# FFN gate and up projections: the low part of a weight chunk formed by an adding transfer instead of by VectorE

## What is computed

```python
def swiglu(h, w_gate, w_up, w_down):
    return (jax.nn.silu(h @ w_gate) * (h @ w_up)) @ w_down
...
        x = x + y
        x = x + swiglu(rms_norm(x, norm_ffn[i]), w_ffn_gate[i], w_ffn_up[i], w_ffn_down[i])
```

## Time and profile before

| what | value |
|---|---|
| time, median of 3 runs | 1503.15 us (1502.79 to 1503.18) |
| span of the profiled execution, first to last instruction | 1500.0 us |
| TensorE busy in the span | 1469.1 us, 98% |
| VectorE, ScalarE, GpSimd busy | 49%, 32%, 14% |
| mean busy share of the 16 DMA engines in a stretch of gate/up (220 to 440 us) | 0.26 |
| granted TensorE clock, mean of the span | 0.993 |

### The profile page before, as it was taken

One profiled execution on the slowest core, in us unless ns is written; L12 is line 12 of the kernel. 1 busy time (PEld: TensorE's weight loads), 2 busy tenths in 40 slices (PEclk: granted clock), 3 DMA queues, 4 the chain that ended last, 5 costly groups with the idle time before them and its releaser, 6 DMA issues.

```text
span 1500.0 us, 28016 instructions
## 1 busy us (share of the span) xinstructions
PE 1469.1 (98%) x11754; PEld 1426.6 (95%) x11754; DVE 728.8 (49%) x867; ACT 475.5 (32%) x547; POOL 208.4 (14%) x209
## 2 busy tenths in 40 slices
PE   6999999999999999999999999989999999999997
PEld 5989999999999999988989989979999999999997
DVE  6564544444443333465574773875444444443223
ACT  3432232222222212254263362463222222221111
POOL 6011130000000112014013041041210000000221
PEclk9999999999999999999999999999999999999998
DMA  6212122222222222555254263333222222222221
GB/s 236 85 61 93 54 88 85 84 97 99 84 75 77 95 97 90 219 175 183 85 204 154 98 232 111 140 140 142 85 99 99 84 84 98 97 66 78 96 97 57
DMA packets 32230, 165.84 MB, mean 111 GB/s; under 512 B 3904, under 2 KB 6224, under 8 KB 20400
## 3 DMA queue, kind: packets, MB, share of 16 engines
q1 hardware_dynamic: 21792, 126.90, 24.3%
q0 software_dynamic: 10384, 38.16, 7.1%
HBM read 140.46 MB, written 24.59 MB: 110 GB/s over the span
## 4 chain that ended last, share of the span: by engine, by line
PE 95%; DVE 2%; ACT 1%; POOL 1%; issue 0%; DMA 0%; DVEq 0%; SPq 0%; ACTq 0%; POOLq 0%
PE ps L1361 83%; PE ax L1722 2%; PE ax L1731 1%; PE ax L1704 1%; PE ps L1862 1%; PE ax L1651 1%; PE ax L1743 1%; PE ax L1379 1%; PE ax L1387 1%; DVE h_lo L711 1%; PE ax L1689 0%; PE ax L1530 0%; POOL acc L1233 0%; PE ax L1499 0%; DMA x<-in_x 0%
## 5 line engine op out<-in xcount | busy, mean ns | idle before, releaser
L1361 PE MATMUL ps<-h_hi,whi 128*128 128x260 f32 x2432 | 496.8, 285 | 1.3 <-DVE wlo L731 1.3
L1361 PE MATMUL ps<-h_hi,wlo 128*128 128x260 f32 x2432 | 491.1, 284 | 0.0
L1361 PE MATMUL ps<-h_lo,whi 128*128 128x260 f32 x2432 | 490.1, 283 | 0.0
L1361 PEld LDWEIGHTS ps<-h_hi,whi 128*128 128x128 f32 x2432 | 376.4, 189 | 8.0 <-issue 4.9
L1361 PEld LDWEIGHTS ps<-h_hi,wlo 128*128 128x128 f32 x2432 | 375.9, 189 | 0.0
L1361 PEld LDWEIGHTS ps<-h_lo,whi 128*128 128x128 f32 x2432 | 375.4, 189 | 0.0
L351 ACT ACTIVATE whi<-raw 128x2048 fp32r<-128x2048 f32 (+1 forms) x119 | 210.6, 1770 | 490.4 <-PE ps L1361 481.9
L706 DVE TENSOR_TENSOR wlo<-raw,whi 128x2048 fp32r<-128x2048 f32 (+1 forms) x119 | 255.5, 2147 | 128.9 <-ACT whi L351 128.7
L722 DVE TENSOR_TENSOR t<-ps,rstd 128x520 f32<-128x520 f32 x108 | 75.5, 699 | 274.8 <-PE ps L1361 269.1
L1361 PE MATMUL ps<-hid_hi,whi 128*128 128x260 f32 x660 | 133.2, 283 | 0.0
L1361 PE MATMUL ps<-hid_hi,wlo 128*128 128x260 f32 x660 | 132.7, 282 | 0.0
(11 more groups left out here) (260 smaller groups left out, 1587.6 us busy)
## 6 DMA issues: line engine op xcount, KB each, us to landing
raw<-in_w_f SPq DMA_DIRECT2D x44, 1024.0 KB, 4.7
raw<-in_w_oi SPq DMA_DIRECT2D x24, 1024.0 KB, 4.7
raw<-in_w_d SPq DMA_DIRECT2D x32, 704.0 KB, 4.0
sring<-in_ret_in POOLq DMA_DIRECT2D x32, 512.0 KB, 4.8
out_ret_s<-sring POOLq DMA_DIRECT2D x32, 512.0 KB, 3.0
raw<-in_w_e SPq DMA_DIRECT2D x8, 1024.0 KB, 4.7
raw<-in_w_oo SPq DMA_DIRECT2D x8, 1024.0 KB, 4.7
raw<-in_w_eo SPq DMA_DIRECT2D x4, 1024.0 KB, 4.7
```

Source lines behind the costliest of these rows:

```text
L1361: ins = pe.matmul(dst[t], lhs(a, kw), rhs[b][:, kx, HT * t:HT * t + HT], start=(first and n == 0 and q == 0), stop=(last and n == len(ks_) ...
```

## The change

For the 20 chunks that are formed inside the gate/up loop of each layer (n = 0 to 19, forming chunks 2 to 21), VectorE's subtraction is left out. ScalarE first writes the negated high part into `wlo` (a copy of `raw` with scale -1, rounded on writing) and after it the high part into `whi`. GpSimd waits for the negated part and issues a transfer that adds `raw` onto `wlo` where it lies, so that `wlo` ends as `raw` minus the high part. VectorE, at the place where it subtracted, waits for that transfer, tells TensorE that the low part is there, and goes on with `hid_lo`. All other chunks keep the subtraction. The core of the diff:

```diff
+        s_neg = sem("ffn_weights_hi_negated")
+        s_sum = [sem(f"ffn_weights_lo{i}_summed") for i in range(2)]
...
                         act.activation(t1[:], t0[:], ACT.Silu).then_inc(s_sg, 1)
+                        if size == W_FULL:
+                            act.wait_ge(s_raw[j], 8 * (c0 + n + 2 - j) + 16)
+                            act.wait_ge(s_mm, m0 + 2 * n + 2)
+                            act.activation(wlo[j][:], raw[j][:], ACT.Copy, scale=-1.0).then_inc(s_neg, 1)
                         hi(c0 + n + 2, j, size, (s_mm, m0 + 2 * n + 2))
...
                         dve.tensor_tensor(t3[:], t2[:], t1[:], ALU.mult).then_inc(s_hid, 1)
-                        lo(c0 + n + 2, j, size)
+                        if size == W_FULL:
+                            dve.wait_ge(s_whi, c0 + n + 3)
+                            dve.wait_ge(s_sum[j], 16 * ((FT // 2 - 1) * l + i + 1))
+                            dve.sem_inc(s_wlo, 1)
+                        else:
+                            lo(c0 + n + 2, j, size)
                         dve.wait_ge(s_hidhi, g + 1)
...
+            def ffn_lo(l):
+
+                with pool.Fori(0, FT // 2 - 1) as i:
+                    for j in range(2):
+                        pool.wait_ge(s_neg, (FT - 2) * l + 2 * i + j + 1)
+                        pool.sem_inc(s_pstep, 1)
+                        pool.dma_start(wlo[j][:].bitcast(F32), raw[j][:], accum_op=ALU.add).then_inc(s_sum[j], 16)
+
             for n, m0 in ((1, M_EO), (2, M_D[0])):
                 for m in range(KT):
                     squares(n, m, (s_out, m0 + m + 1))
+                if n == 1:
+                    ffn_lo(0)
...
+                if n == 3:
+                    ffn_lo(1)
```

## The result

The changed kernel takes **1509.28 us** (median of 8, 1504.85 to 1510.27), the kernel before 1503.29 (median of 8, 1502.79 to 1504.70): a ratio of 1.0030, 95% interval 1.0021 to 1.0039. It is slower, by 6 us in the medians where 19 were forecast (the changed kernel's executions spread over 5.4 us; the means, 1508.16 and 1503.46, are 4.7 apart, and the ratio lies nearer to theirs). Of the kernels further down, one execution of the late wait (2396.86 us) and one of negation first (3672.16 us) lie far above all others; the medians in the table hold them and the ratios do not. The profiled execution took 1504.99 us with a span of 1503.5, so 1.5 us lie around the span.

The account below looks back on a forecast made before the run. TensorE, busy 98% of the span, was taken to bound the kernel. A ring of 12.02 us against 11.54 over 40 chunks gave +19 on the 1500.0 span, 1519, plus 3.15 to the median: 1522 us, range 1501 to 1600.

Parts of the forecast that it names:

- What bounds the kernel, and what the removal buys: In gate/up TensorE alone bounds, 11.54 us per chunk; removing 92 us of VectorE subtractions buys nothing.
- The ring: Gate/up loop per chunk: negating copy, GpSimd, transfer, hid_lo, gate tile, SiLU; 4.62 us + X against TensorE's 11.54.
- X: Adding transfer's time from issue to landing in gate/up; free up to 6.92 us, beyond that 40 us per us.
- I take 7.4: Chosen adding-transfer time in us, a quarter of the way from 6.9 to 9.0; 0.48 over per chunk, +19 us.
- my middle line: Adding transfer with second read at the first's pace: 6.9 us; ring 11.52, a hair under TensorE's 11.54.
- hidden: Rival: adding transfer in gate/up takes at most 7.0 us and costs nothing; 1503 us, chance 33%.
- 7.3 us of slack: Before the change, VectorE's low part in gate/up is ready 7.3 us before TensorE wants the slot again.
- No margin at all: Argument against the hidden rival: the ring at 6.9 just fits, and hand-overs counted at 0.03 us may be more.
- the likeliest case: The ring binds in gate/up, X between 7.0 and 9.0 us; 1506 to 1586, likeliest 1522; chance 50%.
- The frame: Around the whole kernel: the runs' median lies 3.15 us above the span, taking 1519 to 1522 us.

Follow-up runs that it names:

- late wait: Changed kernel with VectorE's wait for the adding transfer moved behind the next chunk's gate tile; 1503.35 us, ratio 1.000 to the kernel before.
- negation first: Changed kernel with ScalarE's negating copy placed ahead of the same chunk's SiLU; 1508.40 us, ratio 1.0038 to the kernel before.
- plain copy: Changed kernel with GpSimd's transfer copying raw over wlo instead of adding; 1506.34 us, ratio 1.0024 to the kernel before; run again 1504.40 us, 1.0009.
- the half: Changed kernel with only 1024 of 2048 columns negated and transferred, VectorE subtracting the others after the wait; 1504.02 us, ratio 1.0009 to the kernel before.
- third-pair kernel: Changed kernel with the first two pairs of chunks of each layer keeping VectorE's subtraction; 1505.13 us, ratio 1.0016 to the kernel before.

## Why the prediction was right and wrong

- **What bounds the kernel, and what the removal buys: right.** The subtractions stood on no path; 92 us less on VectorE quickened nothing, and the late-wait kernel, which has the same relief, is at 1.000.
- **The ring: right in its path and its slope; its length is right partly by luck.** TensorE waits for the gate tile, and adding 0.53 us to the ring cost 20 us. Without X it was put at 4.62, and it measures 11.56 - 6.93 = 4.63. But the parts are off in both directions: from the landing to `hid_lo` it takes 0.26 us, not the 0.03 borrowed from a hand-over between VectorE and ScalarE, and against that GpSimd wakes 0.05 sooner, and `hid_lo` and SiLU let the next instruction begin 0.08 and 0.09 ahead of their end. The prediction named such overlaps as a way to be wrong.
- **The step that failed is "I take 7.4".** I put X a quarter of the way from 6.9 to 9.0, for operands that wait on each other and for more to describe. X measured 6.93 (6.88 to 7.02 where nothing delays it): the second read at the pace of the first, my middle line. There is indeed more to describe (0.86 us of issue against 0.54 for the plain copy), but 6.93 contains it. Each tenth of X weighs 4 us here, so the half microsecond made the 19. The rule of the Trainium skill's page "Collectives: The Full Stack", section "The bandwidth ceiling: the fold count and why AG ≠ RS ≠ AR", that an add costs no time of its own but a second read, is stated there for a reducing collective; here the 6.93 and the half's 2.4 per half MB agree with it.
- **The rival *hidden* failed too, at the same X.** With X = 6.9 it gave 1503. Two things it left out made 4.1 to 5.2 us of FFN. The ring at 6.93 is 11.56, not 11.52: 0.02 to 0.1 over in every chunk. The two long pieces of the chain hold 2.0 us of it: 335.21 - 334.62 and 320.13 - 318.70, the second numbers at the pace of the earlier trace rows. The negation-first kernel, which removes it, has 2.7 left of 4.75. And the first transfers come late once, with code fetches in their flight (that these delay them is argued above) and from one late wake-up of GpSimd: about 2.7 us (the third-pair kernel, which removes the fetches' part, has 2.1 left). Before, a low part that came 1.5 us late would have lost itself in 7.3 us of slack. "No margin at all" was in the text, but only the steady part was priced; single late transfers stood at nothing, without a reason.
- **That 1509 lies in the likeliest case's range, 1506 to 1586, is luck.** The condition of that case, X of 7.0 or more, is not met. At X = 6.93 the prediction's own ring is 11.55, 0.01 over TensorE's period, and gives less than 1504; the further hundredths in every chunk (2.0 us) and the late first transfers (2.7 us) made up the rest.
- **The frame was right in size, not in its reason.** Around the span lie 1.5 us and not 3.15; the profiled execution of before was some 1.7 us quicker than the median.
- **Not settled:** up to some 1.5 us that lie outside the FFNs (0.37 of it is GpSimd's closing instruction), why the clock is lower in some executions of the changed and of the negation-first kernel, GpSimd's late wake-up, and why its closing takes 3 us longer in the plain copy.

No version beats the kernel before: with TensorE busy throughout, the best that freeing VectorE gives is 1.000.

## What to carry to other kernels

Before a wait goes into an in-order list, walk on from it through the engines until you come back, add up that loop, and set it against the period of the engine that bounds: what is over it is paid in every turn. A loop that just fits is not free either, since each single delay (a code fetch, a late wake-up) is then paid in full. What it needs to spare is the largest single delay, here some 1.5 us: with 0.65 us to spare the negation-first kernel still lost 2.7 us, with some 2 us the half and the late wait lost next to nothing. Or move the wait behind what the bounding engine needs next, as the late wait did. Check every hand-over against a row of its own kind, since errors that cancel here need not cancel elsewhere. Price an adding transfer by two reads, and do not add a margin that no row shows to a term that is multiplied by forty.

## What the runs showed of the hardware

- An adding transfer between two tiles on the chip, issued by GpSimd, took 6.93 us for 1 MB and 4.5 for 512 KB; the plain copy of 1 MB took 4.5. Its 8 KB packets took 642 ns in the median, against 328 for those of the plain copy. GpSimd was busy 0.86 us with each issue, 0.54 with the plain copy's.
- A transfer over 16 DMA engines is as late as its latest engine: with a 16 KB packet of program code in its flight, fifteen reported by 6.93 us and the last at 8.44. Of 22 adding transfers of 1 MB with such a packet 18 landed after 7.15 us or more, of 282 without one none after more than 7.11.
- VectorE's `hid_lo` began 0.26 us after the landing that it waited for, while ScalarE's SiLU began 0.03 us after the end of VectorE's gate tile (in layer 1 0.03 and 0.11 in turn).
- GpSimd took 0.57 to 0.73 us from ScalarE's end to its issue, and with adding transfers once in layer 1 1.35 to 1.40, at a place that moved when its loop began later; the two plain-copy profiles have 0.59 at that place. The cause was not found.
